# Gated DeltaNet heads: o squared ahead of the last take, 18 pieces ahead of q's sum, w_ada's fourth group behind the third

## What is computed

```python
mod = silu(cond) @ w_ada + b_ada                  # shift, scale, gate, each 2048 wide
h = rmsnorm(x, g_pre) * (1 + scale) + shift
qa, ka, va, za, ga, ba, ... = split(h @ w_in)     # one wide input projection
q, k, v = split(silu(centred_dwconv(concat(qa, ka, va))))
q, k = l2norm(q), l2norm(k)
o = gdn_chunked(q, k, v, g0, beta0, s0) + flip(gdn_chunked(flip(q), flip(k), flip(v), g1, beta1, s1))
out_a = rmsnorm(o, gdn_norm) * silu(za)           # 4 heads of gated DeltaNet
# beside it: 8 heads of latent attention, 4 heads of mLSTM
x = x + gate * rmsnorm(concat(out_a, out_b, out_c) @ w_out, g_post)
```

## Time and profile before

| | us |
|---|---|
| median of 3 runs | 3296.64 (3293.19 to 3300.91) |
| the profiled execution | 3291.37 |
| its span, first to last instruction | 3289.6 |
| PE busy | 3092.9 (94%) |
| POOL busy | 2069.7 (63%) |
| DVE busy | 1223.9 (37%) |
| ACT busy | 826.0 (25%) |
| mean granted clock of TensorE | 0.984 of full speed |

### The profile page before, as it was taken

One profiled execution on the slowest core, in us unless ns is written; L12 is line 12 of the kernel. 1 busy time (PEld: TensorE's weight loads), 2 busy tenths in 40 slices (PEclk: granted clock), 3 DMA queues, 4 the chain that ended last, 5 costly groups with the idle time before them and its releaser, 6 DMA issues. The chain is left out here.

```text
span 3289.6 us, 64727 instructions
## 1 busy us (share of the span) xinstructions
PE 3092.9 (94%) x27490; PEld 2788.4 (85%) x27490; DVE 1223.9 (37%) x2462; ACT 826.0 (25%) x1698; POOL 2069.7 (63%) x2507
## 2 busy tenths in 40 slices
PE   6899999999999999999997999999999999999996
PEld 1488888889999997879986988889999999787996
DVE  1245545532322113442127447655333311345112
ACT  1323423411111213331005224433111122233000
POOL 3184434546666887446877735544777788653886
PEclk9999999999999999999998999999999999999998
DMA  8523433414444221113222322321222222111322
GB/s 321 198 91 109 139 106 104 138 63 132 127 135 135 77 71 65 35 45 104 74 76 102 112 71 92 101 93 60 78 84 86 88 72 73 54 39 37 115 77 112
DMA packets 122034, 319.93 MB, mean 97 GB/s; under 512 B 18256, under 2 KB 27600, under 8 KB 120592
## 3 DMA queue, kind: packets, MB, share of 16 engines
q1 hardware_dynamic: 91008, 263.38, 25.0%
q10 hardware_dynamic: 30736, 52.40, 4.6%
HBM read 302.65 MB, written 13.08 MB: 96 GB/s over the span
## 5 line engine op out<-in xcount | busy, mean ns | idle before, releaser
L489 POOL TENSOR_SCALAR w_hi<-raw 128x256 fp32r<-128x256 f32 x1232 | 1067.9, 892 | 1160.9 <-PE projection L589 673.7
L494 POOL TENSOR_TENSOR w_lo<-raw,w_hi 128x256 fp32r<-128x256 f32 x1232 | 952.0, 803 | 0.0
L587 PE MATMUL projection<-h_hi,w_hi 128*128 128x320 f32 x2304 | 763.5, 331 | 6.9 <-ACTq L1323 3.9
L589 PE MATMUL projection<-h_hi,w_lo 128*128 128x320 f32 x2304 | 715.0, 310 | 0.1
L588 PE MATMUL projection<-h_lo,w_hi 128*128 128x320 f32 x2304 | 714.1, 310 | 0.2 <-issue 0.2
L534 PE MATMUL projection<-h_hi,w_hi 128*128 128x320 f32 x1984 | 616.2, 311 | 20.7 <-POOLq L499 18.5
L535 PE MATMUL projection<-h_lo,w_hi 128*128 128x320 f32 x1984 | 613.7, 309 | 0.0
L536 PE MATMUL projection<-h_hi,w_lo 128*128 128x320 f32 x1984 | 613.5, 309 | 0.0
L587 PEld LDWEIGHTS projection<-h_hi,w_hi 128*128 128x128 f32 x2304 | 435.9, 189 | 47.6 <-issue 41.2
L588 PEld LDWEIGHTS projection<-h_lo,w_hi 128*128 128x128 f32 x2304 | 436.6, 189 | 0.5 <-issue 0.5
L589 PEld LDWEIGHTS projection<-h_hi,w_lo 128*128 128x128 f32 x2304 | 434.7, 189 | 0.7 <-issue 0.7
(11 more groups left out here) (399 smaller groups left out, 4306.5 us busy)
## 6 DMA issues: line engine op xcount, KB each, us to landing
raw<-in_w_stream SPq DMA_DIRECT2D x308, 512.0 KB, 3.3
fill<-in_w_fill SPq DMA_DIRECT2D x256, 256.0 KB, 2.7
work<-in_w_ada SPq DMA_DIRECT2D x64, 512.0 KB, 5.0
work<-rows ACTq DMA_DIRECT2D x32, 320.0 KB, 4.1
xo<-rows ACTq DMA_DIRECT2D x32, 320.0 KB, 5.0
xo<-in_x ACTq DMA_DIRECT2D x1, 5120.0 KB, 16.7
work<-in_x ACTq DMA_DIRECT2D x16, 320.0 KB, 5.2
x_kept<-xo ACTq DMA_DIRECT2D x4, 1280.0 KB, 4.5
```

The source lines that it names most:

```text
L489: nc.gpsimd.tensor_scalar(w_hi[:, s, cs, :], raw[:, s, cs, :], 1.0, None, ALU.mult).then_inc(split_part, 1)
L494: nc.gpsimd.tensor_tensor(w_lo[:, s, cs, :], raw[:, s, cs, :], w_hi[:, s, cs, :].bitcast(F32), ALU.subtract).then_inc(split_part, 1)
L587: mm(o, w_hi[:, half, c, :], h_hi[:, k, hs], start=(k == 0), stop=False)
L589: last = mm(o, w_lo[:, half, c, :], h_hi[:, k, hs], start=False, stop=(k == KT - 1))
```

## The change

Three pieces of order, in the queues of PE and ACT; no instruction is added or left out.

1. In layer 0, PE's `group(3, ...)`, `turned(2)` and `turned(3)` are moved from behind the first 8 gate cells to directly behind group 2.
2. In each head of gated DeltaNet, PE takes 18 cells ahead of q's sum (before: 16) and 7 behind the q-k product (before: 9).
3. In each such head, ACT squares o ahead of the take of tile 3 instead of behind it.

```diff
--- before.py
+++ after.py
@@ -684,14 +684,14 @@
                     group(2, range(4))
                     turned(1)
                     group(2, range(4, KT))
+                    group(3, range(4))
+                    turned(2)
+                    group(3, range(4, KT))
+                    turned(3)
                     Q.wait("act", "rstd")
                     Q.leave()
                 gate_cells(range(KT // 2))
                 if l == 0:
-                    group(3, range(4))
-                    turned(2)
-                    group(3, range(4, KT))
-                    turned(3)
                     A.note()
                     pe.wait_ge(s_ada.sems["dve"], s_ada.total["dve"])
                     pe.sem_inc(fill_ready, 1)
@@ -724,7 +724,7 @@
                     B = s_gdn.body("pe", pe, l * H_A + h)
 
                     ahead = Ahead(B, int(l * STREAM_HALVES + h * 8 + (STREAM["gates"] + 8)), 4)
-                    ahead.cells(16)
+                    ahead.cells(18)
                     B.wait("act", "q squared")
                     B.did(column_sums(wa, wt(9)), "q sum")
                     ahead.cells(1)
@@ -742,7 +742,7 @@
                     B.did(each_tile(wa, wt(1), wt(1)), "kk")
                     B.wait("dve", "q normed")
                     B.did(each_tile(wb, wt(1), wt(0)), "qk")
-                    ahead.cells(9)
+                    ahead.cells(7)
 
                     def block_of(ap):
                         return lambda t: ap[:, t * BLOCK:(t + 1) * BLOCK]
@@ -1261,9 +1261,9 @@
                             for d in range(2):
                                 B.wait("dve", f"state{d}0")
                                 act.dma_start(io["new_gdn"][l, d, h, :, :], gdn_final(d)).then_inc(state_out[d], 16)
-                    take(B, n0_, 3, xt(7))
                     B.wait("dve", "o whole")
                     B.did(A(wt(6), wt(4), ACT.Square), "o squared")
+                    take(B, n0_, 3, xt(7))
                     B.wait("pe", "o sum")
                     rsqrt(B, wt(7), wa[:, 0:TOK], wt(7), 1.0 / P, "o rstd")
                     for d in range(2):
```

## The result

The changed kernel takes 3292.06 us (median of 13 runs, 3284.72 to 3294.91), the kernel before 3295.99 in as many runs beside them: 0.9984 times, with an interval of 0.9977 to 0.9991. That is 3.9 us less, or no change by the bound of 0.2%. The forecast was 3279.5 us in a range of 3271 to 3288: the time lies outside. Some 13 us of the 17.1 that the sum gave didn't come.

The account below looks back on a forecast made before the run. TensorE, busy for nearly the whole span, was taken as the bound, so time moves only where it waits or its work is stretched; 5.1 + 13.5 - 1.5 = 17.1 us off 3296.6 gave 3279.5 us, range 3271 to 3288.

Parts of the forecast that it names:

- Part 1: Layer 0's last w_ada group: tiles come 5.6 us sooner, less 0.5 for GpSimd's later half; gain 5.1 us, bounds 2 and 7.2.
- The rival of a lower clock in the start-up: Group 3 leaves TensorE at 1.2 GHz, so the first part costs 3.4 us instead of giving 5.1; 3288.0 us, chance 0.04.
- Part 2: End of each head: o's square ahead of the last take saves 1.69 us in eight heads, 13.5 us, bounds 10.4 and 15.2.
- the square isn't earlier: Rival at a head's end: "o whole" comes late, so the early square gives nothing; 3293.0 us, chance 0.04.
- The slower rival, longer unreleased waits: At the block products each of 23 waits grows to 2.3 us, 28.7 us more in all; 3308.2 us, chance 0.02.
- part 3's term, -1.5 us: 18 and 7 pieces: q waits filled, mask waits in layer 1, net -2.2, taken as -1.5 us; bounds -5 and +2.
- The waits at the masks in layer 0: Sign of a wrong forecast: TensorE waiting for the inverse's first masks in layer 0, where none was expected.
- the prediction's own four heads: Layer 1: q's sum 1.8 us later against mask covers of 0.62, 0.05, 0.38 and 0.37 us; sum -2.2 us.
- What I wrote off against unreleased waits: Waits in front of block products, 24.2 us in 23, can shorten, so the loss of 2.2 us was taken as 1.5.
- q's chain decides in every head: Rival: nothing covers q's later sum, costing 8 x 1.95 = 15.6 us against 18.6; 3293.6 us, chance 0.05.
- layer 0's 2.5 us of cover: Layer 0's second mask ends 2.5 us before TensorE wants it, against 2.1 us of delay: nothing or near nothing lost.

Follow-up runs that it names:

- part 1 alone: Kernel before with only layer 0's fourth w_ada group moved directly behind the third; 16 and 9 pieces and the late square stay: 3290.55 us, ratio 0.999.
- parts 1 and 2 alone: Changed kernel with 16 and 9 pieces again instead of 18 and 7, also called without part 3: 3272.28 us, ratio 0.9931 to the kernel before.
- The kernel with a shorter chain: Changed kernel with VectorE's multiplication of each direction's decay by beta left out, so the result isn't the reference's: 3272.56 us, ratio 0.9935 to the kernel before.
- 20 and 5 pieces: Changed kernel with 20 pieces ahead of q's sum instead of 18 and 5 behind q-k instead of 7: 3310.12 us, ratio 1.0047 to the kernel before.
- the control: Kernel with the w_ada move and early square but 16 and 9 pieces, with the multiplication by beta left out: 3266.55 us, ratio 0.9921 to the kernel before.
- the kernels with 17 or 18 pieces and 9 ahead of the masks: Changed kernel with 9 pieces behind q-k; 17 ahead of q's sum and 3 behind the diagonal blocks: 3275.19 us; 18 and 2: 3275.45 us.
- part 3 alone: Kernel before with only 18 pieces ahead of q's sum and 7 behind q-k instead of 16 and 9: 3309.34 us, ratio 1.0044.

## Why the prediction was wrong

**What held.** Part 1: its chain went step by step as worked out, though the last tile came 6.9 us sooner and not 5.6, and 4.8 us arrived where 5.1 was forecast, with an interval that ends at no change. The rival of a lower clock in the start-up fell: behind `turned(3)` the granted clock was 1.00 until 153.1 us, and in the trace of part 1 alone, where it was 1.2 GHz for 6.8 us from 135.6 on, it rose again. Part 2: the wait left for the take is 0.54 us in layer 0 and 0.28 in layer 1 (0.1 or nothing in each layer's last head) where some 0.4 was forecast, 12.6 us of idle time went where 13.5 was, and 17 came out; "the square isn't earlier" fell. The slower rival, longer unreleased waits, fell too: at the block products (both rows of L613) they are 24.5 to 29.0 us in all fourteen traces.

**What failed: part 3's term, -1.5 us, which was -14 alone and -19 beside the other two.** The step that failed is the time of the masks: it took VectorE's way to them as fixed and found layer 0 covered, and it priced a wait at its length alone. The waits at the masks in layer 0, named as a sign of being wrong, came. In detail:

*The masks don't keep their distance from q.* I moved q's sum by 1.8 us and left VectorE's chain as long as it was. Here are VectorE and then GpSimd in head 1 of layer 0, before:

```profile
390.20 0.25 DVE L1661 TENSOR_SCALAR column_temps<-token_columns 128x5 f32<-128x5 f32 x1
...
390.56 0.16 DVE L1663 TENSOR_TENSOR column_temps<-xo,column_temps 128x5 f32<-128x5 f32 x1
390.75 0.82 DVE L1665 TENSOR_TENSOR work<-xo,column_temps 128x640 f32<-128x640 f32 x1
...
399.11 0.82 DVE L1682 TENSOR_TENSOR xo<-xo,constants 128x640 f32<-128x640 f32 x1
```

```profile
387.96 4.33 POOL L489 TENSOR_SCALAR w_hi<-raw 128x256 fp32r<-128x256 f32 x4 [5.36 <-PE projection L589]
392.26 3.60 POOL L494 TENSOR_TENSOR w_lo<-raw,w_hi 128x256 fp32r<-128x256 f32 x4
```

and after, in the same order:

```profile
386.02 0.58 DVE L1661 TENSOR_SCALAR column_temps<-token_columns 128x5 f32<-128x5 f32 x1
...
386.71 0.58 DVE L1663 TENSOR_TENSOR column_temps<-xo,column_temps 128x5 f32<-128x5 f32 x1
387.32 1.33 DVE L1665 TENSOR_TENSOR work<-xo,column_temps 128x640 f32<-128x640 f32 x1
...
395.62 1.01 DVE L1682 TENSOR_TENSOR xo<-xo,constants 128x640 f32<-128x640 f32 x1
```

```profile
380.53 3.56 POOL L489 TENSOR_SCALAR w_hi<-raw 128x256 fp32r<-128x256 f32 x4 [5.62 <-PE projection L589]
384.06 3.91 POOL L494 TENSOR_TENSOR w_lo<-raw,w_hi 128x256 fp32r<-128x256 f32 x4
392.99 3.41 POOL L489 TENSOR_SCALAR w_hi<-raw 128x256 fp32r<-128x256 f32 x4 [5.02 <-PE projection L589]
396.37 2.95 POOL L494 TENSOR_TENSOR w_lo<-raw,w_hi 128x256 fp32r<-128x256 f32 x4
```

GpSimd's half is released by a piece (the bracket: PE projection L589). With 18 pieces ahead, that piece comes before v's transposes and no longer behind them, so GpSimd's four subtractions (L494), from 384.06 to 387.97, now lie on VectorE's steps L1661 to L1666; before, they lay behind these, from 392.26. The three rows of VectorE took 0.25, 0.16 and 0.82 us and take 0.58, 0.58 and 1.33. The next half comes sooner too and meets the masks. From v's transposes to the second mask's end it was 13.71 us in layer 0 and is 15.02; in layer 1 13.90 became 15.02 to 15.57. In the kernel before one head of layer 1 had 14.35. In layer 0 the first block product started 15.86 us after v's transposes and now starts 14.14 after them, with 0.54 us of waiting for the first mask in that and 0.37 more for the second behind it: 0.91 in a head, 3.6 in the layer. By the old chain, 13.71, neither would have been a wait. The second mask in layer 1's heads (minimum/median/maximum ns), first changed, then parts 1 and 2 alone:

```profile
L1682 DVE TENSOR_TENSOR xo<-xo,constants x4: 1015/1352/1355, 1887.4 to 2235.0; 128x640 f32<-128x640 f32 x4
```

```profile
L1682 DVE TENSOR_TENSOR xo<-xo,constants x4: 1017/1018/1019, 1881.0 to 2219.0; 128x640 f32<-128x640 f32 x4
```

The Trainium skill, "SBUF — State Buffer", section "Who interferes with whom", has an exclusion between a VectorE instruction with two SBUF inputs and a GpSimd instruction that reads SBUF. The two TENSOR_TENSOR rows agree. The prediction had weighed it for part 1, where it cost almost nothing, and not for part 3, where it decided layer 0. The kernel with a shorter chain shows the weight of the chain's length: the same order of pieces, 17.4 us better. That GpSimd is what lengthens it rests on these rows, which repeat in all eight heads of five traces to a few hundredths of a us; no run moved GpSimd's split alone.

*The price of layer 1.* On an unchanged chain the prediction's own four heads give some 5.8 us of mask waits (four times 1.8, less the covers of 0.62, 0.05, 0.38 and 0.37), against which I set the 3.5 us of q waits that go. That is right in kind, but both numbers moved: the mask waits are 10.2 us, and beside part 2 only 2.2 us of q waits were left to fill. What I wrote off against unreleased waits, 0.7 us, did come: at the block products they are 25.1, 26.7 and 24.7 us in three traces of the changed kernel, 29.0 and 27.2 in two without part 3.

*No clock cost.* I priced idle time at its own length. Head 1 of layer 1, the block products behind the mask wait, and the stretches ahead of, at and behind it:

```profile
2003.27 0.76 PE L613 MATMUL wa<-constants,work 128*32 128x32 f32 x40 [2.11 <-DVE work L1682]
2004.54 0.77 PE L613 MATMUL wb<-constants,xo 128*32 128x32 f32 x40 [0.51 <-DVE xo L1682]
```

```profile
1999.90:2003.20 3.30, 1.26 (x9) 0.99 (x7) 3.20 (x6) 0.56 (x1) 3.30 (x5) 1.00 0.55 209
2003.20:2010.00 6.80, 6.22 (x178) 5.60 (x179) 4.18 (x8) 5.90 (x18) 3.26 (x4) 0.50 0.15 38
2010.00:2015.00 5.00, 5.00 (x252) 4.34 (x253) 2.90 (x7) 1.31 (x5) 0.00 (x0) 1.00 0.03 7
```

TensorE was busy for 1.26 of 3.30 us and then got 1.2 GHz for 6.8 us, in which 40 block products took 0.76 us; without part 3, at the full clock, 38 of them took 0.53. The same head without part 3 has no wait, and the clock stays up:

```profile
1992.50:1995.00 2.50, 2.50 (x85) 2.31 (x85) 1.83 (x4) 1.05 (x4) 2.22 (x2) 1.00 0.92 303
1995.00:2002.00 7.00, 6.84 (x300) 5.99 (x287) 5.02 (x10) 7.00 (x22) 4.48 (x7) 1.00 0.18 46
```

In the means over runs the clock loss is 53.1 us with part 3 and 46.4 without: 6.7 us. The traces say the same: some 13 us more at 1.2 GHz, half of which is lost.

*The fill bursts.* With two more pieces ahead, a burst is wanted sooner than its weights have come. The waits are 3.4, 1.7 and 3.8 us in three traces of the changed kernel and 1.6 and 2.5 in two without part 3: 0.9 us in the means, no more than the scatter. Only with 20 and 5 pieces, 6.5 us, do they stand out.

Together, in means over these traces: 14.1 us of mask waits, less 2.2 of q waits and 2.6 of unreleased waits, 0.9 for the bursts and 6.7 for the clock are 16.9 us, and 19.2 were measured, with an uncertainty of some 4 us. The stretches that hold the waits (in each layer from v's transposes in the first head to the first matmul of the stage behind the last) take 888.1, 883.4 and 885.5 us together in the changed kernel's traces and 873.3 and 870.9 in those without part 3, 13.6 us more. Where the rest of the 19.2 lies isn't shown.

**The rivals.** "q's chain decides in every head" gave 3293.6, nearly the measured time, in part by luck. Its point was right that layer 0's 2.5 us of cover don't hold, its mechanism only half: layer 0 paid 3.6 us and not 8.4, as the cover was eaten by VectorE's longer chain; the rest are layer 1's waits and the clock. I gave it 5 in 100, because I read the cover from a chain that the change itself would lengthen.

**Not settled.** Why part 2 gave 17.0 us, with 15.6 accounted for; the 4 us that the control gained; the last 4 to 5 us of the kernels with 17 or 18 pieces and 9 ahead of the masks. None is larger than the intervals.

## What to carry to other kernels

When pieces of filler move from one wait to another, the wait at the new end has to be worked out from the engine that releases it, with everything else that those pieces release: here a piece freed GpSimd's next half, and GpSimd slowed the VectorE chain for which TensorE then waited. Look at the smallest cover along the whole chain (here 0.05 to 0.62 us in layer 1), not at the wait to be filled; waits of up to 1.8 us at q were exchanged for up to 2.8 at the masks. And moving an instruction ahead of another whose input comes later (part 2) is the cheap kind of change: it adds no work ahead of anyone, and of a wait of 2.1 us it left 0.5. Not tried: computing the first masks ahead of the q-k products (L1676), on which they don't depend.

## What the runs showed of the hardware

- A VectorE instruction on 128x5 elements took 0.58 us instead of 0.16 to 0.25 beside GpSimd's subtractions, and one on 128x640 took 1.33 instead of 0.82. The small ones lost most for their size.
- TensorE's granted clock fell to 1.2 GHz at eight of the nine places in three traces of the changed kernel where it stood 2.6 to 2.9 us for masks, ahead of block products of 32 rows. Behind the waits of 1.7 to 2.1 us for o's square, between dense pieces, it fell less often: two of eight in the kernel before and with part 1 alone, three of eight with part 3 alone (and once each, in the first two, at a wait of 1.8 us for q's square). Whether the length of the wait or the thin work behind it makes the difference no run shows; in the changed kernel's first trace two of the drops begin within 0.1 us of the wait's end. The loss is not in the table of waits; it shows only in the clock column and in longer durations of the same instruction.
- The start-up isn't steady: the same first memset of the gates stage was at 150.8, 155.6 and 156.5 us in three executions of the changed kernel.
